# First shift's turns half a chunk later, and forgetting gates of the heads from column tiles

## The chip, the cores and the metric

One core of a Trainium2 chip runs the whole program as a single launch. The metric is the device time of that launch in microseconds (us). TensorE (PE) multiplies matrices into PSUM; ScalarE (ACT), VectorE (DVE) and GpSimd (POOL) do the element work; SyncE (SP) issues the loads of the weights. All data is float32.

## The reference, cut to what matters

256 tokens of width 1024 pass through two blocks of two layers each. The first block's first layer is a differential-attention mixer with a SwiGLU; its activations are shifted and scaled by vectors that come from a conditioning vector `c`:

```
mod_l = split(silu(c) @ ada_w[i] + ada_b[i], 6)     # shift, scale, gate (mixer); shift, scale, gate (ffn)
x = x + mod_l[2] * mixer(...)
x = x + mod_l[5] * swiglu(rmsnorm(x) * (1 + mod_l[4]) + mod_l[3])
```

In the second block each of the two layers has a mixer over one wide projection `h = rms_norm(x) @ w_mix_in` with 3336 columns. The last eight columns are the forgetting logits of the eight attention heads:

```
(..., h_q, h_f, ..., f_q, f_k, f_v, f_f) = split(h)
log_f = log_sigmoid(f_f + f_bias);  cum = cumsum(log_f over tokens)
logit[t, s] = q_t . k_s + cum_t - cum_s              # causal softmax over s
```

The same mixer has an HGRN2 part (`h_q`, `h_f`, ...) whose gates are worked out from 256-column slices of `h`.

## The kernel before, in words

**Products.** Weights stream as 1 MB slabs of 128 x 2048 into a ring of five raw buffers. For each slab ACT makes a rounded copy `hi` (L1277) and DVE the rest `lo` (L1793); both sit in rings of four. PE multiplies activations (also split, `XTh` and `XTl`) with them three times (L458 to L460). A "half chunk" is one slab: four row tiles, two token tiles, three products, 24 matmuls of 512 columns. Each engine's order of work is written out by hand, and the engines wait for each other by semaphores only.

**The first layer's conditioning.** Products of `c` with `ada_w` come as slabs of a quarter matrix. For some (`ada_slab`, L476) PE does them itself with the two columns of `CS` as standing weights, in four column tiles of 32 (L484). For the others (`ada_quarter`, L1809) DVE sums them into `ROW`, eight instructions for a half (L1827, L1830), and PE turns each half of `ROW` into columns by eight matmuls on a matrix of ones (`half_turn`, L505, L517 holds the matmul: four of them, of two passes each). DVE then adds the bias (`half_mods`, L1834, L1842), which frees the next `half_turn` (L511). Half 1 of shift (0, 3) waits for half 0's `half_mods`. The order on PE around the first of these, shift (0, 3), in chunk c == 4 of the first projection, is L622 to L639: the half chunk d+8, both half turns, an `ada_slab`, the half chunk d+9, an `ada_slab`, then the turns of keys and queries (`heads`, L556). On DVE it is L2005 to L2011: two quarters of `ROW`, two `half_mods`, three small instructions (`factor`), and the copy out of PSUM `from_x(4)`.

**The mixer of the second block.** `mix` (PE L1139, ACT L1672, DVE L2467) runs twice. After the first chunk, PE makes the forgetting logits (L1143 to L1147): for each token tile the activations `FULL` (128 x 128) are loaded as standing weights and eight columns of `WF` pass, eight row tiles, so 16 matmuls of eight columns in float32. DVE scales them, adds the bias (L2482), and takes minimum and absolute value (L2486, L2487). Then come the half chunks s = 2 to 11 with small work between. After s == 2 `hgrn_turn` (L1024) turns two slices of `h`; ACT and DVE wait for it (L1685, L2490) and start the chain of the gates (table loads, exponentials, logarithms), which ends for the heads in `LOGS` (L2514). After s == 4 PE sums these over the tokens (`fox_decay`, L1015). `SG` is a buffer that is free at this place; `SEL` (L404, L2356) is a 128 x 8 mask with a one where the partition number mod 32 is the head.

Of the kernel before, what the change touches and what calls it, by code (L numbers as in the profile page):

```python
# [20 lines left out]
P = 128  # L21
D = 1024
KD = D // P
T = 2
# [46 lines left out]
    "hg_decays": "hg_dec hg_tail",  # L71

    "row_squares": "sq sq2 sq_in std std2",
    "exponents": "lam_exp lb_exp",
    "diff_squares": "diff_sq diff_std",
    "hg_logs": "hg_e hg_ln hg_sig hg_z",
    "hg_squares": "hg_rows hg_sq hg_std hg_silu",
# [7 lines left out]
class Counts:  # L85
# [12 lines left out]
    def up(self, name, key=0, step=1):  # L98
        assert (name, key) not in self.table, (name, key)
        shared = SEMAPHORE.get(name, name)  # L100
        self.n[shared] = self.n.get(shared, 0) + step
        self.table[name, key] = self.n[shared]
        return self.sem(name), step

    def at(self, name, key=0):
        return self.sem(name), 1 if self.known is None else self.known[name, key]


def row_tiles(w):
    return w.rearrange("(k p) n -> p k n", p=P)  # L110
# [175 lines left out]
def program(nc, A, out, known):  # L286

    ctx = ExitStack()
    with ctx:
# [4 lines left out]
        def tile_at(name, shape, offset, dt=F32):  # L294
            return nc.alloc_sbuf_tensor_at(name, list(shape), dt, offset=offset)
# [109 lines left out]
        OG = tile_at("OG", [P, HD], gate_at + 11648)  # L405
        FB = tile_at("FB", [P, FOX_H], gate_at + 11904)
        GS = tile_at("GS", [P, T, HALF], gate_at + 11968)
        WF = tile_at("WF", [P, KD, FOX_H], gate_at + 14016)
        FST = tile_at("FST", [P, T, 16], gate_at + 14272)
        LB = tile_at("LB", [P, 8, 2], gate_at + 14528)  # L410
        TRI = tile_at("TRI", [P, 2, P], cst_at)
# [39 lines left out]
        def tensor_engine(pe):  # L451
# [167 lines left out]
            for c in (2, 3, 4):  # L619

                ctx_groups = [(bank[2 + t], CTXh, CTXl, t) for t in range(T)]
                pe.wait_ge(*at("uc_act", (c - 1 if c > 2 else 0, "x")))  # L622
                pe.wait_ge(*at("uc_dve", (c - 1 if c > 2 else 0, "x")))
                half_chunk(d + 2 * c, 0, x_groups_in, False)
                if c == 4:
                    for h in range(2):
                        half_turn(0, 3, h, bank[6])
                    pe.wait_ge(*at("gate_full", (0, 2, 1)))
                    ada_slab(0, 4, 0, bank[7])
                half_chunk(d + 2 * c + 1, 1, x_groups_in, False).then_inc(*up("x_pass", c))  # L630
                if c == 4:
                    ada_slab(0, 4, 1, bank[7])
                    pe.wait_ge(*at("roped", 1280))
                    pe.wait_ge(*at("heads_act", 5))
                    heads(7, bank[4])
                    pe.wait_ge(*at("uc_act", (3, "c")))
                    pe.wait_ge(*at("uc_dve", (3, "c")))
                    pe.wait_ge(*at("heads_act", 6))
                    heads(8, bank[5])  # L639
                if c == 2:  # L640
                    pe.wait_ge(*at("c_hi", 3))
                    pe.wait_ge(*at("c_lo", 3))
                pe.wait_ge(*at("uc_act", (c - 1, "c" if c > 2 else "x")))
                pe.wait_ge(*at("uc_dve", (c - 1, "c" if c > 2 else "x")))
                half_chunk(d + 2 * c, 0, ctx_groups)
                if c == 4:
                    pe.wait_ge(*at("row", (0, 4, 0)))
                    ada_slab(0, 4, 2, bank[7])
                if c == 2:
                    pe.wait_ge(*at("roped", 256))  # L650
                    for n in (0, 1):
                        heads(n, bank[4 + n])
                if c == 3:
                    pe.wait_ge(*at("roped", 768))
                    heads(3, bank[4])
                    heads(4, bank[5])
                    pe.wait_ge(*at("heads_act", 2))
                    half_gate(0, 2, 0, bank[6])
                    half_gate(0, 2, 1, bank[7])
                if c == 4:  # L660
                    pe.wait_ge(*at("heads_act", 8))
                    diff_scores(0)
                half_chunk(d + 2 * c + 1, 1, ctx_groups)
                if c == 4:
                    ada_slab(0, 4, 3, bank[7])
                if c == 2:
                    pe.wait_ge(*at("roped", 512))
                    heads(2, bank[6])
                if c == 3:
                    pe.wait_ge(*at("roped", 1024))  # L670
                    pe.wait_ge(*at("heads_act", 4))
                    heads(5, bank[4])
                    heads(6, bank[5])
                if c == 4:
                    pe.wait_ge(*at("uc_act", (4, "x")))
                    pe.wait_ge(*at("uc_dve", (4, "x")))
                    diff_scores(1)
# [461 lines left out]
            def mix(p):  # L1139
                l, d = MIXES[p], first[f"up{p}"]  # L1140
                first_chunk(p)
                pe.wait_ge(*at("small2", (l, 2)))
                for t in range(T):  # L1143
                    for k in range(KD):
                        last = pe.matmul(bank[7][:, t * FOX_H:(t + 1) * FOX_H], FULL[:, k, tok[t]], WF[:, k, :],
                                         start=(k == 0), stop=(k == KD - 1))
                last.then_inc(*up("fox_z", l))  # L1147
                for s in range(2, 12):
                    c = s // 2
                    if s % 2 == 0 and c >= 2:  # L1150
# [4 lines left out]
                    half_chunk(d + s, s % 2, x_groups(c))  # L1155

                    if s == 2:
                        hgrn_turn(l)
                    elif s == 4:
                        fox_decay(l)  # L1160
                        pe.wait_ge(*at("hg_z", l))
                        pe.wait_ge(*at("hg_k2t", l))
                        hgrn_products(l, 0, K2, Q2, 4)
                    elif s == 6:
                        pe.wait_ge(*at("fox_c", l))
                        hgrn_level(l, 1)
                    elif s >= 7:
                        hgrn_level(l, s - 5)
# [99 lines left out]
        def scalar_engine(act):  # L1268
# [403 lines left out]
            def mix(p):  # L1672
# [6 lines left out]
                                   ACT.Identity, scale=ST[:, 0:1]).then_inc(*up("um_act", (l, c)))  # L1679

                first_chunk(p)
                act.wait_ge(*at("rstd2", p))
                rows_of(0)
                split(d + 5)
# [98 lines left out]
        def vector_engine(dve):  # L1783
# [683 lines left out]
            def mix(p):  # L2467
# [8 lines left out]
                first_chunk(p)  # L2476
                dve.wait_ge(*at("rstd2", p))
                rows_of(0)
                dve.wait_ge(*at("fox_z", l))
                dve.wait_ge(*at("small2", (l, 2)))  # L2480
                for t in range(T):
                    dve.scalar_tensor_tensor(out=FZ[:, 0, t, :], in0=bank[7][:, t * FOX_H:(t + 1) * FOX_H],  # L2482
                                             scalar=ST[:, t:t + 1], in1=FB[:, :], op0=ALU.mult,
                                             op1=ALU.add).then_inc(*up("fox_bias", (l, t)))
                dve.wait_ge(*at("fox_bias", (l, 1)))
                dve.tensor_scalar(FZ[:, 1, :, :], FZ[:, 0, :, :], 0.0, None, ALU.min)  # L2486
                dve.scalar_tensor_tensor(out=FZ[:, 2, :, :], in0=FZ[:, 0, :, :], scalar=-1.0, in1=FZ[:, 0, :, :],  # L2487
                                         op0=ALU.mult, op1=ALU.max).then_inc(*up("fox_abs", l))
                split(d + 5)
                dve.wait_ge(*at("hg_turned", l))  # L2490
                dve.wait_ge(*at("lb", 8))
                dve.tensor_copy(Q2[:, :, :], bank[4][:, :].rearrange("p (k s) -> p k s", k=2)).then_inc(*up("hg_q2t", l))
# [128 lines left out]
        def gpsimd_engine(pool):  # L2621
# [21 lines left out]
            for l in range(2):  # L2643
# [9 lines left out]
                                0.0).then_inc(*up("reset"))  # L2653
                else:
                    pool.wait_ge(*at("added", (5, 1)))
                pool.dma_start(WF[:, :, :], row_tiles(A["w_mix_in_2"][l, :, :])[:, :, MIX_IN - FOX_H:MIX_IN]).then_inc(
                    *up("small2", (l, 0), 16))
                pool.dma_start(FB[:, :], A["fox_f_bias_2"][l, :].partition_broadcast(P)).then_inc(*up("small2", (l, 1), 16))
                pool.dma_start(OG[:, :], A["hgrn_out_gain_2"][l, :].partition_broadcast(P)).then_inc(*up("small2", (l, 2), 16))
# [171 lines left out]
```

## Time and profile before

| | us |
|---|---|
| three runs | 1786.42, 1785.92, 1782.88 (median 1785.92) |
| the profiled execution | 1782.81 |
| its span, first to last instruction | 1781.5 |
| PE busy in the span | 1698.9 (95%) |
| DVE busy | 1104.0 (62%) |
| ACT busy | 807.2 (45%) |
| POOL busy | 48.0 (3%) |

The span is what the trace covers; 1.3 us lie around it. A row of the trace gives start, length, engine, line, operation, output and inputs, the number of instructions merged, and in brackets how long the engine had been idle and what released it. A float32 matmul shows as two records, one for each pass, so a count of records is twice the number of matmuls. The mean granted clock of TensorE over the span is 0.989 of full speed.

### The profile page before, as it was taken

To read this page: it belongs to the slowest core of one execution; us is meant where nothing else is said; L and a number is where in the kernel's file an instruction comes from. 1 tells how busy PE (TensorE), PEld (TensorE's weight loads), DVE (VectorE), ACT (ScalarE), POOL (GpSimd) and SP (SyncE) were. 2 spreads that over 40 slices of the span, in tenths; PEclk is the share of its full clock that TensorE was granted. 3 is DMA by queue.
4 is the path that set the end of the run, shared out by engine and by line. 5 is a ranking of instruction groups with operands and counts; after the bars stand their busy time and mean duration, and the time that the engine had idled before them with its cause. 6 is when DMAs were issued, how large, how long until landed. Compare 5 with 4: busy or idle time off the path is not lost.

```text
span 1781.5 us, 20857 instructions
## 1 busy us (share of the span) xinstructions
PE 1698.9 (95%) x8192; PEld 1375.8 (77%) x8192; DVE 1104.0 (62%) x1284; ACT 807.2 (45%) x968; POOL 48.0 (3%) x60
## 2 busy tenths in 40 slices
PE   6999899999988999999999999999999999999999
PEld 3775678877656887788788788887888788888877
DVE  2876787878657664655546856554655458855542
ACT  3415554333444443464435565443444346664441
POOL 0001000000000000000001200000000003000000
PEclk9999999999989999999999999999999999999999
DMA  9683279887444765565455427655565454336550
GB/s 355 205 279 123 84 257 307 282 293 268 146 135 139 251 233 180 165 194 186 182 165 153 155 72 214 189 188 172 184 189 186 170 168 163 119 99 213 186 187 25
DMA packets 239985, 332.29 MB, mean 187 GB/s; under 512 B 11024, under 2 KB 191988, under 8 KB 239888
## 3 DMA queue, kind: packets, MB, share of 16 engines
q1 hardware_dynamic: 235872, 321.95, 54.4%
q10 hardware_dynamic: 2704, 5.82, 0.9%
q0 software_dynamic: 1312, 3.19, 0.7%
q8 instruction: 66, 1.08, 0.2%
q14 instruction: 31, 0.25, 0.0%
HBM read 329.87 MB, written 1.05 MB: 186 GB/s over the span
## 4 chain that ended last, share of the span: by engine, by line
PE 83%; DVE 10%; ACT 3%; issue 2%; DMA 1%; SPq 0%; DVEq 0%; ACTq 0%
PE bank L458 16%; PE bank L460 16%; PE bank L459 16%; PE bank L789 7%; PE bank L790 7%; PE bank L792 7%; DVE lo L1793 4%; PE bank L887 2%; ACT hi L1277 1%; DMA raw<-in_ada_w 1%; PE bank L1221 1%; PE bank L1222 1%; PE bank L1224 1%; DVE ROW L1830 1%; PE bank L772 1%
## 5 line engine op out<-in xcount | busy, mean ns | idle before, releaser
L1793 DVE TENSOR_TENSOR lo<-raw,hi 128x2048 fp32r<-128x2048 f32 x258 | 591.3, 2295 | 378.9 <-ACT hi L1277 378.6
L1277 ACT ACTIVATE hi<-raw 128x2048 fp32r<-128x2048 f32 x258 | 491.6, 1911 | 333.3 <-PE bank L460 173.8
L458 PE MATMUL bank<-hi,XTh 128*128 128x512 f32 (+1 forms) x1424 | 565.7, 397 | 11.6 <-DVE XTl L1880 4.6
L460 PE MATMUL bank<-hi,XTl 128*128 128x512 f32 (+1 forms) x1424 | 554.1, 389 | 0.0
L459 PE MATMUL bank<-lo,XTh 128*128 128x512 f32 (+1 forms) x1424 | 553.3, 389 | 0.0
L458 PEld LDWEIGHTS bank<-hi,XTh 128*128 128x128 f32 x1424 | 269.2, 189 | 74.3 <-ACT XTh L1293 8.4
L460 PEld LDWEIGHTS bank<-hi,XTl 128*128 128x128 f32 x1424 | 268.6, 189 | 56.4
L459 PEld LDWEIGHTS bank<-lo,XTh 128*128 128x128 f32 x1424 | 269.4, 189 | 52.9 <-issue 1.0
L789 PE MATMUL bank<-hi,HTh 128*128 128x512 f32 x528 | 208.6, 395 | 9.3 <-DVE HTl L1880 9.3
L790 PE MATMUL bank<-lo,HTh 128*128 128x512 f32 x528 | 207.0, 392 | 0.0
L792 PE MATMUL bank<-hi,HTl 128*128 128x512 f32 x528 | 163.5, 391 | 0.0
L789 PEld LDWEIGHTS bank<-hi,HTh 128*128 128x128 f32 x528 | 100.0, 189 | 31.4 <-DVE HTl L1880 10.9
L792 PEld LDWEIGHTS bank<-hi,HTl 128*128 128x128 f32 x528 | 99.7, 189 | 21.1
L790 PEld LDWEIGHTS bank<-lo,HTh 128*128 128x128 f32 x528 | 100.0, 189 | 20.5
L1558 ACT ACTIVATE SG<-bank,ST 128x256 f32<-128x256 f32 x88 | 36.9, 470 | 136.5 <-PE bank L460 136.5
L1830 DVE SCALAR_TENSOR_TENSOR ROW<-raw,CS,ROW 128x512 f32<-128x512 f32 x126 | 94.6, 751 | 4.2
L1293 ACT ACTIVATE XTh<-FULL 128x512 fp32r<-128x512 f32 x44 | 27.4, 632 | 105.7 <-DVE FULL L2160 67.2
L2230 DVE SCALAR_TENSOR_TENSOR HID<-bank,ST,SG 128x256 f32<-128x256 f32 x88 | 38.5, 478 | 55.6 <-ACT SG L1558 55.6
L1880 DVE TENSOR_TENSOR HTl<-bank,HTh 128x512 fp32r<-128x512 f32 x66 | 45.1, 684 | 9.1 <-ACT HTh L1538 9.1
L1558 ACT ACTIVATE SG<-bank 128x256 f32<-128x256 f32 x44 | 14.5, 382 | 71.2 <-PE bank L460 71.2
L1538 ACT ACTIVATE HTh<-bank 128x512 fp32r<-128x512 f32 x66 | 38.5, 583 | 16.3 <-PE bank L887 16.3
L2673 POOL TENSOR_TENSOR hg_e<-hg_BC 128x256 f32<-128x256 f32 x12 | 23.2, 1934 | 641.2 <-DVE hg_BC L2523 620.9
(360 smaller groups left out, 1415.5 us busy)
## 6 DMA issues: line engine op xcount, KB each, us to landing
raw<-in_ffn_w_in SPq DMA_DIRECT2D x176, 512.0 KB, 4.8
raw<-in_ffn_w SPq DMA_DIRECT2D x132, 512.0 KB, 4.9
raw<-in_ada_w SPq DMA_DIRECT2D x96, 512.0 KB, 4.9
raw<-in_ffn_w_out SPq DMA_DIRECT2D x88, 512.0 KB, 4.0
raw<-in_w_mix_in SPq DMA_DIRECT2D x52, 512.0 KB, 4.6
raw<-in_od_pw_w SPq DMA_DIRECT2D x24, 512.0 KB, 4.6
raw<-in_ev_w_in SPq DMA_DIRECT2D x20, 512.0 KB, 9.0
raw<-in_w_mix_out SPq DMA_DIRECT2D x16, 512.0 KB, 4.1
```

Source lines behind the costliest of these rows:

```text
L458: pe.matmul(dst, xh, wh, start=start, stop=False)
L459: pe.matmul(dst, xh, wl, start=False, stop=False)
L460: return pe.matmul(dst, xl, wh, start=False, stop=stop)
L789: pe.matmul(acc[t][m][:, :], sh, w[m][0], start=begin, stop=False)
L790: pe.matmul(acc[t][m][:, :], sh, w[m][1], start=False, stop=False)
L792: last = pe.matmul(acc[t][m][:, :], sl, w[m][0], start=False, stop=end)
L1277: act.activation(hi[r][:, :], raw[g % RAW][:, :], ACT.Copy).then_inc(*up("hi", d))
L1538: act.activation(HTh[:, 2 * c:2 * c + 2, :], b[:, :].rearrange("p (k s) -> p k s", k=2), ACT.Copy).then_inc(*up("ht_hi", (f, c)))
L1558: act.activation(SG[:, t, :], bank[2 * (c % 2) + t][:, 0:HALF], ACT.Silu, scale=1.0 if p in SHIFTED else ST[:, t:t + 1]).then_inc(*up("gat ...
L1793: dve.tensor_tensor(lo[r][:, :], raw[g % RAW][:, :], hi[r][:, :].bitcast(F32), ALU.subtract).then_inc(*up("lo", d))
L1830: m = dve.scalar_tensor_tensor(out=part, in0=w[:, k, :], scalar=CS[:, kk, 0:1], in1=part, op0=ALU.mult, op1=ALU.add)
L1880: dve.tensor_tensor(dst, src, h.bitcast(F32), ALU.subtract).then_inc(*up(name, i))
```

## The change

Three edits. (1) In chunk 4 of the first projection the two half turns of shift (0, 3) stand behind the half chunk d+9 and the `ada_slab` after it, instead of ahead of both; they are still in the same order on DVE. (2) The forgetting logits are made the other way round: eight columns of weights stand still (the tile `CS`, 32 columns wide, of which eight are loaded and 24 are left from before), 256 tokens pass, and row tile k goes to column tile k % 4, so the eight partial products lie in four groups of 32 partitions. ACT copies this 128 x 256 result to `SG`; after the half chunk s == 2 two matmuls with `SG` standing and `SEL` passing sum the four groups and turn tokens to partitions. (3) The instructions of DVE that read the logits move behind the split of slab d+5.

```diff
@@ semaphores
-    "exponents": "lam_exp lb_exp",
+    "exponents": "lam_exp lb_exp fox_zrow",
@@ tiles
-        WF = tile_at("WF", [P, KD, FOX_H], gate_at + 14016)
+        WF = CS
@@ PE, first projection, c == 4
                 half_chunk(d + 2 * c, 0, x_groups_in, False)
                 if c == 4:
-                    for h in range(2):
-                        half_turn(0, 3, h, bank[6])
                     pe.wait_ge(*at("gate_full", (0, 2, 1)))
                     ada_slab(0, 4, 0, bank[7])
                 half_chunk(d + 2 * c + 1, 1, x_groups_in, False).then_inc(*up("x_pass", c))
                 if c == 4:
                     ada_slab(0, 4, 1, bank[7])
+                    for h in range(2):
+                        half_turn(0, 3, h, bank[6])
                     pe.wait_ge(*at("roped", 1280))
@@ PE, mix
                 pe.wait_ge(*at("small2", (l, 2)))
-                for t in range(T):
-                    for k in range(KD):
-                        last = pe.matmul(bank[7][:, t * FOX_H:(t + 1) * FOX_H], FULL[:, k, tok[t]], WF[:, k, :],
-                                         start=(k == 0), stop=(k == KD - 1))
-                last.then_inc(*up("fox_z", l))
+                for k in range(KD):
+                    o = 32 * (k % 4)
+                    last = pe.matmul(bank[7][o:o + 32, 0:S], WF[:, k, :], FULL[:, k, :], start=(k < 4), stop=(k >= 4),
+                                     tile_position=(0, o))
+                last.then_inc(*up("fox_parts", l))
...
                     if s == 2:
+                        pe.wait_ge(*at("masks"))
+                        pe.wait_ge(*at("fox_zrow", l))
+                        for t in range(T):
+                            last = pe.matmul(bank[7][:, S + t * FOX_H:S + (t + 1) * FOX_H], SG[:, 0, tok[t]],
+                                             SEL[:, :].bitcast(F32), start=True, stop=True)
+                        last.then_inc(*up("fox_z", l))
                         hgrn_turn(l)
@@ ACT, mix
                 first_chunk(p)
+                act.wait_ge(*at("fox_parts", l))
+                act.activation(SG[:, 0, :], bank[7][:, 0:S], ACT.Copy).then_inc(*up("fox_zrow", l))
                 act.wait_ge(*at("rstd2", p))
@@ DVE, mix
                 rows_of(0)
+                split(d + 5)
                 dve.wait_ge(*at("fox_z", l))
                 dve.wait_ge(*at("small2", (l, 2)))
                 for t in range(T):
-                    dve.scalar_tensor_tensor(out=FZ[:, 0, t, :], in0=bank[7][:, t * FOX_H:(t + 1) * FOX_H],
+                    dve.scalar_tensor_tensor(out=FZ[:, 0, t, :], in0=bank[7][:, S + t * FOX_H:S + (t + 1) * FOX_H],
...
-                split(d + 5)
@@ POOL
-                pool.dma_start(WF[:, :, :], row_tiles(...)[:, :, MIX_IN - FOX_H:MIX_IN])
+                pool.dma_start(WF[:, :, 0:FOX_H], row_tiles(...)[:, :, MIX_IN - FOX_H:MIX_IN])
```

## Rows read from the trace of the kernel before

**Rows 1.** The page: the chain that ended last, shares by engine

```profile
PE 83%; DVE 10%; ACT 3%; issue 2%; DMA 1%; SPq 0%; DVEq 0%; ACTq 0%
```

**Rows 2.** Timeline of 118 to 136 us, first layer

```profile
118.40 5.54 DVE L1830 SCALAR_TENSOR_TENSOR ROW<-raw,CS,ROW 128x512 f32<-128x512 f32 x7
...
118.71 0.95 PE L517 MATMUL bank<-ONES,ROW 128*128 128x2 f32 x8
...
123.86 0.15 DVE L1842 TENSOR_TENSOR MODS<-bank,COLS 128x4 f32<-128x4 f32 x1
...
124.09 1.85 PE L517 MATMUL bank<-ONES,ROW 128*128 128x2 f32 x8 [4.44 <-DVE MODS L1842]
...
125.87 1.94 PE L484 MATMUL bank<-raw,CS 128*32 128x512 f32 x8
...
134.31 1.06 PE L484 MATMUL bank<-raw,CS 128*32 128x512 f32 x8
135.30 0.66 PE L562 MATMUL bank<-IDENT,UROW 128*128 128x128 f32 x4
```

**Rows 3.** Stretches: us, busy time of PE, PEld, DVE, ACT, POOL, granted clock, DMA share, GB/s

```profile
118.70:124.00 5.30, 0.95 (x9) 0.86 (x7) 5.02 (x8) 0.00 (x0) 0.00 (x0) 0.89 0.72 230
124.00:127.70 3.70, 3.61 (x16) 1.99 (x16) 0.46 (x5) 0.00 (x0) 0.00 (x0) 0.50 1.04 350
127.70:129.70 2.00, 2.00 (x9) 1.58 (x6) 0.00 (x0) 0.00 (x0) 0.00 (x0) 0.52 0.57 164
...
154.00:200.00 46.00, 40.59 (x243) 28.20 (x243) 33.84 (x79) 31.12 (x88) 3.64 (x7) 1.00 0.17 53
```

**Rows 4.** SP's queue at 110 us, and the page's issues (KB, us to landing)

```profile
110.28 0.88 SPq L2696 DMA_DIRECT2D raw<-in_ada_w  x2
...
raw<-in_ada_w SPq DMA_DIRECT2D x96, 512.0 KB, 4.9
```

**Rows 5.** Timeline of the first mixer, 948 to 961 us

```profile
948.85 3.74 PE L1145 MATMUL bank<-WF,FULL 128*128 128x8 f32 x32
949.11 0.69 ACT L1678 ACTIVATE UM<-bank,ST 128x512 f32<-128x512 f32 x1 [0.73 <-PE bank L460]
...
952.44 0.77 PE L458 MATMUL bank<-hi,XTh 128*128 128x512 f32 x1
...
959.51 1.03 PE L1031 MATMUL bank<-IDENT,UM 128*128 128x128 f32 x8
...
960.58 0.69 DVE L2492 COPY hg_Q<-bank 128x512 f32<-128x512 f32 x1 [5.11 <-PE bank L1031]
```

**Rows 6.** Timeline of the second mixer, 1465 to 1476 us

```profile
1465.69 3.63 PE L1145 MATMUL bank<-WF,FULL 128*128 128x8 f32 x32
...
1469.18 0.49 PE L458 MATMUL bank<-hi,XTh 128*128 128x512 f32 x1
...
1474.77 1.04 PE L1031 MATMUL bank<-IDENT,UM 128*128 128x128 f32 x8
```

**Rows 7.** Stretches of the mixers, columns as in Rows 3

```profile
952.40:955.60 3.20, 3.20 (x9) 2.52 (x10) 2.81 (x5) 0.00 (x0) 0.00 (x0) 0.50 0.91 315
...
1469.20:1474.50 5.30, 5.30 (x25) 4.38 (x25) 2.81 (x5) 0.00 (x0) 0.00 (x0) 1.00 0.76 231
```

**Rows 8.** Timeline, PE, 454 to 456 us: 16 records of 256 columns in four tiles

```profile
454.63 1.11 PE L973 MATMUL bank<-TAPW,TAPD 31*81 31x256 f32 x16
455.67 0.50 PE L458 MATMUL bank<-hi,XTh 128*128 128x512 f32 x1
```

**Rows 9.** Timeline of ACT at 973 us: a copy of 128 x 256 out of PSUM

```profile
972.91 0.36 ACT L1706 ACTIVATE NCT<-bank 128x256 fp32r<-128x256 f32 x1
```

**Rows 10.** Timeline at 970 to 972 us: the logs of the gates and their first reader

```profile
970.60 0.41 DVE L2514 TENSOR_TENSOR LOGS<-FZ 128x256 f32<-128x256 f32 x1
...
971.28 0.39 PE L1020 MATMUL bank<-TRI,LOGS 128*128 128x128 f32 x2
```

**Rows 11.** Small work of DVE on the logits, first mixer

```profile
952.62 0.36 DVE L2482 SCALAR_TENSOR_TENSOR FZ<-bank,ST,FB 128x8 f32<-128x8 f32 x2 [1.17 <-PE bank L1145]
```

More of the change, by code:

```diff
@@ L2655, in gpsimd_engine @@
                     pool.wait_ge(*at("added", (5, 1)))
-                pool.dma_start(WF[:, :, :], row_tiles(A["w_mix_in_2"][l, :, :])[:, :, MIX_IN - FOX_H:MIX_IN]).then_inc(
+                pool.dma_start(WF[:, :, 0:FOX_H], row_tiles(A["w_mix_in_2"][l, :, :])[:, :, MIX_IN - FOX_H:MIX_IN]).then_inc(
                     *up("small2", (l, 0), 16))
```

## The prediction

> **What bounds the kernel now.** I read the page first. The chain of work that ended last is PE for 83% and DVE for 10%, and DMA for 1% [rows 1]: PE's instructions in order, broken by short stretches in which another engine is late. So PE time removed counts in full if nothing else is late afterwards, and loads matter little. Then I read the timeline around the two places of the change and the stretches with their granted clock. (About 0.2% of the time, 3.6 us, is what a measurement of this kernel can tell from no change.)
>
> At the first place PE ends half 0's turn (118.71 plus 0.95) and then stands for 4.44 us until DVE's bias add at 123.86 [rows 2]. DVE is not slow at that add, it takes 0.15; it is queued behind the sums of the other half of ROW, 5.54 us from 118.40 [rows 2]. When PE goes on, the clock is at its lower level, 1.2 GHz: 0.50 over 124.0 to 127.7 and 0.52 over 127.7 to 129.7, after 0.89 in the stretch that holds the stand [rows 3]. Everything there costs nearly double: half 1's turn 1.85 against 0.95, a slab product 1.94 against 1.06 [rows 2].
>
> At the second place, twice, PE makes the logits in 32 records (16 matmuls of two passes), from 948.85 to the next chunk's first matmul at 952.44, and from 1465.69 to 1469.18, so 3.59 and 3.49 us [rows 5, 6]. That is 0.109 us a record with only eight columns: loading the 128 x 128 of FULL as weights sets it. In the first mixer the clock is then at 0.50 for 3.2 us, in the second it stays at 1.00 [rows 7], and the chunk behind takes 959.51 less 952.44, 7.07, against 1474.77 less 1469.18, 5.59 [rows 5, 6].
>
> **Edit 1, the half turns moved.** Old, from half 0's turn to the turns of keys: 135.30 less 118.71, 16.59 us [rows 2]. New, in PE's new order at full clock: slab product 0.99 (134.31 to 135.30), half chunk 5.59 (the one at full clock, rows above), slab product 0.99, half 0's turn 0.95, the wait for DVE, half 1's turn 0.95 [rows 2, 6]. The wait: DVE began its add at 123.86 and PE went on at 124.09, 0.23 [rows 2]; DVE is free from 123.86 and half 0 now ends near 127.2, so it is waiting already, with 3.4 us to spare. The bounds of this wait are 0.23 and the old 4.44; I take 0.27. Sum 9.74, **gain 6.85**: of it 4.2 is the stand and the rest the low clock.
>
> Queued behind DVE's adds is from_x(4), which used to run as soon as the half chunk was done and now comes after both, some 3.5 us later relative to that chunk. Its reader is the second pair of scores, after two more half chunks, so it is covered by over 11 us. ACT's copy of ROW now waits for half 0's turn; it is read after the next half chunk, covered too. The first slab product is asked for at 118.7 instead of 125.87: its load was issued at 110.28 and the median landing of such a load is 4.9 [rows 2, 4], so it lands near 116. The slab then frees 7 us sooner and SP issues the next one sooner; SP's queue is in order and nobody is hurt. What is late next? After this place comes attention, where PE, ACT and DVE release each other and the DMA share is 0.17 over 154 to 200 us [rows 3]. No load that was begun before holds a clock of its own there, so the whole sequence should start and end earlier by the same amount.
>
> **Edit 2, the logits by column tiles.** Removed: 3.59 and 3.49. Added: eight matmuls of 256 columns, 16 records in four tiles. The nearest row has this count and width, in row tiles: 16 records of 256 columns from 454.63 to 455.67, **1.04** [rows 8]. The column tiles of the first layer are 8 records of 512 columns in 0.99 [rows 2], the same columns in all, with the same four tiles. Bounds: 0.99 if columns count, 1.98 if records count, and 4.0 if the tiles do not overlap (a 512 wide matmul lasts about 0.99, half of that eight times). I take 1.04 and 0.1 for going in and out of tiles. Added after s == 2: two matmuls, four records with full weights and eight columns, 4 times 0.109, **0.44** [rows 6]. The Trainium skill (TensorEngine Tiling (Array Packing), Instruction Overhead) puts a fixed cost of about 60 cycles on a matmul, whatever its columns below that; by it alone, an estimate, four records would be 0.1 us. The row has four times that for this very shape, and it decides.
>
> Second mixer: 3.49 less 1.14 less 0.44, **gain 1.9**. First mixer: 3.59 less 1.58 is 2.0, and the chunk behind falls from 7.07 to 5.59, 1.48 more, if the clock stays up because the thin stretch of 3.6 us in front of it is gone: **gain 3.5**. Whether it stays up the rows of before can't say; bounds 2.0 and 3.5.
>
> **ACT, DVE, POOL there.** ACT gets one copy of 128 x 256, 0.36 [rows 9], between its last split and the rows of the first chunk. It used to be free for those rows at 949.11 less 0.73 [rows 5]; it now waits for the partial sums until about 950.0, so rows and the next split come some 1.3 us later. The readers of the rows (hgrn_turn) come after 955, the split is for a chunk three chunks away. Its cost is nothing while that cover holds, and 1.3 without it. PE's wait for the copy is 5 us after it. DVE's logits work now starts when the two small matmuls end and runs beside hgrn_turn, which is 1.03 long; the first step takes 0.36 [rows 5, 11] and two shorter ones follow, so DVE is ready when the turn is, where it had idled 5.11 [rows 5]. The split of slab d+5 goes ahead of it and fills that idle time; it ends about 955.0, before the logits at 955.7. The POOL load of the weights has the same pieces into another tile, long before use: nothing.
>
> Does the gain go on from hgrn_turn? ACT and DVE start their gate chain from that turn, and its end, LOGS at 970.60 plus 0.41, meets PE at 971.28, 0.27 us of slack [rows 10]. Both sides start at the same turn, so both move by the same amount and the slack remains. Were the gates started later than the turn, PE would wait here.
>
> **Sum.** 6.85 + 3.5 + 1.9 = 12.25. The profiled execution has 1782.81 (span 1781.5 and 1.3 around it), which gives 1770.6; the median of the runs shown is 3.1 higher, so I forecast **1773.6**.
>
> **Rivals.**
>
> *A, the clock falls all the same.* In edit 1 the two turns (two columns each) and the turns of heads now stand together, 0.95 + 0.27 + 0.95 + some 1.0, a stretch as thin as the logits of the first mixer, after which the clock fell in one of two mixers [rows 7]. If it falls there, a half chunk costs 1.48 more; if it also falls in the first mixer (the small matmuls and the transposes of hgrn_turn, 1.5 us), 1.48 again. Time 1773.6 + 3.0 = 1776.6. Against it: no stand remains, and 256 column products replace the thin ones. Chance 0.16.
>
> *B, column tiles do not overlap for two rounds.* The second round adds onto the same 32 columns, and its weights can enter only when the first lets them. 4.0 instead of 1.04, twice: 1773.6 + 5.9 = 1779.5. The row of four row tiles in two rounds speaks against it [rows 8]. Chance 0.06. The skill (TensorEngine Tiling (Array Packing), Key Properties) adds that a change of tiling mode drains the engine. The trace agrees as far as it can: the tiled group of rows 8 costs 1.04 with its way in and out, so a drain is a tenth and not a microsecond.
>
> *C, edit 1's gain is taken back in the first feed-forward*, where PE, the sums of ROW on DVE and the loads all run close together. If that stage ends when its loads end and those don't start sooner, 6.85 is lost: 1780.4. Against it: its loads start only when PE and the splits free slabs, and attention in between leaves DMA at 0.17 [rows 3]. Chance 0.10. It is still faster by 5.4, 0.3%.
>
> *D, slower.* The place is the end of s == 2 in each mixer: PE stands for ACT's copy, which is in ACT's queue behind a split that waits for its slab. A stand there moves hgrn_turn and with it the gate chain, which has 0.27 to spare [rows 10], and is followed by a stretch of low clock. It decides if the copy comes over 5 us after the partial sums; to end slower than before the stands and their low clock must come to over 6 us in each mixer: 1788. ACT has been free since 948.4, so chance 0.02.
>
> *E, nothing to be seen*: both A and C, and part of B, 1783 to 1786. Chance 0.04.
>
> **How the numbers follow.** The forecast has 0.62. Its own range is 1768 to 1777: 3.1 down if the runs fall where the profiled execution fell, 2 more if stretches of low clock elsewhere fall otherwise, and as much up. A and C are taken in, and B nearly, to 1780; the range 1767 to 1780 leaves out B's end, D and E. Faster by over 0.2%: forecast, A, B and C, 0.94; within 0.2%: 0.04; slower: 0.02.
>
> **What the trace after would show.** Right: the idle time before the second group of turns is near 0.2 instead of 4.44, clock 1.00 from 118 to 136; turns of keys near 128.4; attention as long as before; L1145 gone for a group of 16 records about 1.04 long and one of 4 records of 0.44; hgrn_turn's end 3.5 us and 1.9 us nearer to the first chunk's end; the gate chain reaches PE with the slack unchanged. Wrong: a clock of 0.50 after the turns (A), a group of 4 us (B), a feed-forward that ends where it ended (C), or an idle row of PE released by ACT's SG (D).

## The result and the profile after

The changed kernel took 1772.63 us in the median of four runs (1771.67 to 1773.08); the kernel before, run beside it, 1784.4 (1781.35 to 1786.42, four runs). The ratio is 0.9934, 95% interval 0.9921 to 0.9947. Forecast were 1773.6 and a range of 1767 to 1780. The profiled execution took 1772.36, its span is 1771.1 against 1781.5.

The page of the changed kernel shows busy time by engine and the chain that ended last. The bound is the same engine:

```profile
PE 1696.4 (96%) x8168; PEld 1370.1 (77%) x8168; DVE 1104.2 (62%) x1284; ACT 807.9 (46%) x970; POOL 48.2 (3%) x60
...
PE 84%; DVE 9%; ACT 3%; issue 2%; DMA 1%; SPq 0%; DVEq 0%; ACTq 0%
```

The timeline of PE at edit 1, against [rows 2] (line numbers are those of the changed kernel; L485 is the slab product; L518 the half turns, four matmuls or eight records for each half; L563 the turns of keys):

```profile
123.06 1.06 PE L485 MATMUL bank<-raw,CS 128*32 128x512 f32 x8
124.05 1.05 PE L518 MATMUL bank<-ONES,ROW 128*128 128x2 f32 x8
125.36 1.05 PE L518 MATMUL bank<-ONES,ROW 128*128 128x2 f32 x8 [0.25 <-DVE MODS L1852]
126.27 0.63 PE L563 MATMUL bank<-IDENT,UROW 128*128 128x128 f32 x4
```

The stand of 4.44 us is now 0.25. The turns of keys begin 9.88 us after the first slab product (116.39 in this trace), forecast 9.74, and the old order took 16.59 [rows 2]. The stretches around it, columns as in [rows 3]:

```profile
116.39:124.05 7.66, 7.66 (x41) 4.74 (x40) 4.93 (x7) 0.60 (x1) 0.00 (x0) 1.00 0.82 273
124.05:126.27 2.22, 1.97 (x20) 1.88 (x17) 0.16 (x1) 0.60 (x1) 0.00 (x0) 1.00 1.01 339
126.27:130.20 3.93, 3.93 (x17) 3.34 (x17) 1.04 (x5) 2.99 (x3) 0.00 (x0) 0.57 1.00 369
```

The clock is full through the turns and then falls to its lower level all the same, in the turns of keys and the half chunk behind them. That is the first half of rival A, and it gives part of the gain back.

The timeline of the first mixer, against [rows 5] (L1147 the products in column tiles, L1163 the two small matmuls, L1032 hgrn_turn):

```profile
944.09 0.59 PEld L1147 LDWEIGHTS bank<-FULL,CS 128*32 128x32 f32 x16 [0.35 <-issue]
944.10 1.07 PE L1147 MATMUL bank<-FULL,CS 128*32 128x256 f32 x16
945.23 0.39 ACT L1691 ACTIVATE SG<-bank 128x256 f32<-128x256 f32 x1 [1.71 <-PE bank L1147]
...
948.13 2.29 DVE L1803 TENSOR_TENSOR lo<-raw,hi 128x2048 fp32r<-128x2048 f32 x1 [1.52 <-ACT hi L1285]
...
950.72 0.51 PE L1163 MATMUL bank<-SEL,SG 128*128 128x8 f32 x4
...
951.08 1.07 PE L1032 MATMUL bank<-IDENT,UM 128*128 128x128 f32 x8
951.26 0.36 DVE L2493 SCALAR_TENSOR_TENSOR FZ<-bank,ST,FB 128x8 f32<-128x8 f32 x2 [0.84 <-PE bank L1163]
...
952.19 0.69 DVE L2502 COPY hg_Q<-bank 128x512 f32<-128x512 f32 x1 [0.28 <-PE bank L1032]
```

Sixteen records of 256 columns in 1.07 (forecast 1.04), four small ones in 0.36 from start to start (forecast 0.44); ACT's copy 0.39; DVE is through with the logits 0.28 before it is needed. From the logits' start to hgrn_turn it is 6.98 us, against 10.66 before [rows 5]; about 0.1 more is spent ahead of the group, where the loads of the tiles' weights start late by 0.35. In the first mixer the next chunk starts 1.00 after the group (945.10). In the second mixer L1147 starts at 1457.26 and L1032 at 1464.24, again 6.98, against 9.08 [rows 6].

Where the 10.45 us of difference between the two spans went can be read by setting the same instructions of both traces side by side. I took the starts of ACT's splits (258 in both; the 9th starts at 99.51 in the trace of before, the 13th at 196.75, the 53rd at 459.80, the 65th at 568.96, the 129th at 942.26, the 133rd at 971.11, the 213th at 1463.32, the 217th at 1488.45). Each number below is the time between two of these splits in the changed kernel less the same time in the trace of before, in us. "<99.5" is the time up to the 9th split, "-197" from there to the 13th, and so on:

```
                       start  edit 1   to   to     to    mixer  mix1 to mixer  to     sum
                       <99.5   -197   460   569    942     1    mixer2    2    end
changed kernel         -2.35  -5.08  0.29  2.06   0.23  -3.54  -0.14  -1.98   0.06  -10.45
```

The forecast was -6.85, -3.5 and -1.9 at the three places. The two mixers fit within 0.1. Two parts were not in the sum: 2.35 less before the first edited instruction, and 2.06 more between 460 and 569 us.

### The profile page after: what moved, and what is told of

It is laid out like the page before. It is cut to its first block, busy times and chain, and to the rows that moved or that the text cites. A ratio compares the mean times of both kernels' runs of the same rounds, so it can differ in the third digit from the quotient of the medians.

```text
span 1771.1 us, 20813 instructions
## 1 busy us (share of the span) xinstructions
PE 1696.4 (96%) x8168; PEld 1370.1 (77%) x8168; DVE 1104.2 (62%) x1284; ACT 807.9 (46%) x970; POOL 48.2 (3%) x60
## 4 chain that ended last, share of the span: by engine, by line
PE 84%; DVE 9%; ACT 3%; issue 2%; DMA 1%; SPq 0%; DVEq 0%; ACTq 0%
PE bank L459 17%; PE bank L461 17%; PE bank L460 17%; PE bank L790 7%; PE bank L793 7%; PE bank L791 7%; DVE lo L1803 3%; PE bank L888 2%; DMA raw<-in_ada_w 1%; ACT hi L1285 1%; PE bank L773 1%; PE bank L1229 1%; PE bank L1230 1%; PE bank L1232 1%; PE bank L950 1%
```

## The experiments

The questions are these. Do the two edits add up, each at its own place? Do the fall of the clock behind the turns and the 2.06 us belong to the change? What do the tiles, the delay of half a chunk and DVE's order bring?

The table for all runs first, so that each can be read against it; "clock low" lists where the granted clock was at its lower level from 100 us on, start and length, as recorded in each trace (stretches from 1766 us on, at the very end, are left out). Every row is set against the one profiled execution of the kernel before, that of the rows. The four f kernels ran once each, with the kernel before once beside them, 1780.85 us, so they are read by their traces.

```
                  start  edit 1   to    to    to    mixer  mix1 to mixer   to    sum    clock low from 100 us on (start, length)
                  <99.5   -197   460   569   942     1    mixer2    2     end
kernel before                                                                           123 6.8; 358 3.4; 369 3.4; 509 10.2; 754 3.4; 952 3.4
changed kernel    -2.35  -5.08  0.29  2.06  0.23  -3.54  -0.14  -1.98   0.06  -10.45    127 3.4; 226 3.4; 352 3.4; 362 3.4; 499 13.7; 550 6.8; 748 3.4
a0_again          -2.40  -3.98  0.36  0.57  0.40  -3.56   0.08  -1.97   0.10  -10.40    128 3.4; 148 3.4; 227 3.4; 353 3.4; 363 3.4; 500 13.7; 749 3.4
a0_third           0.75  -6.63 -0.01  0.48  0.27  -3.54  -0.12  -1.96   0.06  -10.71    353 3.4; 363 3.4; 500 13.7; 749 3.4
e1_turns_only     -1.19  -5.09  0.38  2.06  0.27  -1.58  -0.16   3.23  -0.02   -2.10    128 3.4; 227 3.4; 353 3.4; 364 3.4; 500 13.7; 551 6.8; 749 3.4; 1463 6.8
e2_logits_only    -2.33  -0.32 -0.04 -0.07  0.22  -3.55   0.11  -1.97   0.08   -7.87    120 6.8; 355 3.4; 366 3.4; 506 10.2; 751 3.4
e3_turns_split     0.60  -7.14  0.41  0.51  0.05  -3.55  -0.10  -1.97   0.07  -11.11    226 3.4; 353 3.4; 363 3.4; 499 13.7; 749 3.4
e3_again          -0.11  -7.20 -0.02  0.45  0.15  -3.52  -0.15  -1.96   0.08  -12.27    351 3.4; 362 3.4; 498 13.7; 747 3.4
e5_turns_ahead    -2.33  -6.77  0.49  0.49 -0.03  -3.53   0.07  -1.97   0.09  -13.48    224 3.4; 350 3.4; 360 3.4; 497 13.7; 746 3.4
e5_again          -0.34  -5.19  0.43  0.60  0.40  -3.55  -0.24  -1.97   0.02   -9.85    129 3.4; 228 3.4; 354 3.4; 364 3.4; 501 13.7; 750 3.4
f1_one_tile       -1.06  -5.04  0.30  2.10  0.08  -0.74   0.03   0.83   0.05   -3.43    128 3.4; 227 3.4; 354 3.4; 364 3.4; 500 13.7; 552 6.8; 750 3.4
f2_sum_behind     0.20  -4.04  0.46  0.46 -0.04  -3.96   0.53  -2.35   0.60   -8.13    130 3.4; 150 3.4; 229 3.4; 355 3.4; 366 3.4; 502 13.7; 751 3.4
f3_sum_at_once    -1.08  -5.08  0.30  2.13  0.13  -2.89   0.06  -1.33   0.03   -7.75    128 3.4; 227 3.4; 354 3.4; 364 3.4; 500 13.7; 552 6.8; 749 3.4
f4_split_back     -2.26  -5.02  0.25  0.69  0.05  -3.55  -0.22  -1.95   0.12  -11.90    127 3.4; 226 3.4; 352 3.4; 362 3.4; 499 13.7; 748 3.4
```

### Edit 1 alone

```diff
@@ kernel before, PE, c == 4
-                    for h in range(2):
-                        half_turn(0, 3, h, bank[6])
                     pe.wait_ge(*at("gate_full", (0, 2, 1)))
...
                     ada_slab(0, 4, 1, bank[7])
+                    for h in range(2):
+                        half_turn(0, 3, h, bank[6])
```

> Edit 1 alone on the kernel before; the logits stay as they were. Theory (the stand of 4.44 us goes, the low clock moves from the half chunk to the turns of heads): about 5 us faster than before, so 1779 or 0.997; PE waits 0.2 to 0.3 us for the first bias add, the clock is at 0.5 for one stretch behind the turns, and the mixers cost what they cost before (3.6 and 3.5 us for the logits, low clock behind the first). Rival (attention or the first feed-forward take the gain back): no difference, 1784.

Measured: 1778.97 (ten runs) against 1784.29, ratio 0.9968 (0.9957 to 0.9979), so 5.3 us less. In the trace edit 1's place is 5.09 shorter and the wait is 0.25, as in the changed kernel. The rival falls: by 460 us 0.38 is taken back, and 2.06 between 460 and 569 us, which still leaves the kernel clearly faster. One part of the expectation missed: the first mixer kept its clock although its logits were the old ones, and the second lost it for 6.8 us. The stretches of the second mixer of this kernel, columns as in [rows 3], the logits and the chunk behind:

```profile
1459.50:1463.20 3.70, 3.70 (x29) 3.54 (x27) 2.96 (x2) 2.90 (x3) 0.00 (x0) 0.94 0.82 275
1463.20:1470.40 7.20, 7.20 (x25) 6.06 (x24) 2.81 (x5) 0.00 (x0) 0.00 (x0) 0.56 0.61 176
```

That costs 3.23 there, and the first mixer is 1.58 shorter than in the trace of before with the same instructions. So the old logits lose the clock in one of the two mixers in both traces, and which one it is changes. None of the twelve profiles with the new logits has a fall in either mixer.

### Edits 2 and 3 alone

```diff
@@ changed kernel, PE, c == 4
+                    for h in range(2):
+                        half_turn(0, 3, h, bank[6])
                     pe.wait_ge(*at("gate_full", (0, 2, 1)))
...
                     ada_slab(0, 4, 1, bank[7])
-                    for h in range(2):
-                        half_turn(0, 3, h, bank[6])
```

> Edits 2 and 3 alone: the half turns stand where they stood. Theory (PE's path in the two mixers is 3.5 and 2.0 us shorter): 5.5 us faster than before, 1779; the stand of 4.4 us and the low clock near 124 us are there as before. Rival (the gate chain or a split is late and takes part back): 2 us or less, with a wait of PE for LOGS or for a slab in the trace.

Measured: 1777.15 (five runs) against the same 1784.29, ratio 0.9961 (0.9946 to 0.9977), 7.1 us less where 5.5 were expected; the interval reaches from 4.1 to 9.6 and holds both. The trace has 3.55 and 1.97 less in the mixers, and the stand is as it was:

```profile
121.77 1.85 PE L518 MATMUL bank<-ONES,ROW 128*128 128x2 f32 x8 [4.50 <-DVE MODS L1852]
```

The rival falls. The places add up: 5.1 (e1_turns_only) and 5.5 (this kernel), against 10.6 in the three places of the changed kernel. This kernel also has the 2.33 less in the first 99.5 us, where no edit of it lies, and it has neither the low clock near 226 us nor more of it near 500, and no extra time there.

### The changed kernel again

> The changed kernel once more. Every theory expects 1772 to 1773 and the turns of keys near 126 us. Open is the feed of low clock between 480 and 560 us, which was 20.5 us long in the profile of the changed kernel and 10.2 in that of before: if it belongs to the change it is there again with the same length, if it is a matter of the single execution it is not.

> The changed kernel, third time, as the measure for the two beside it. Every theory expects 1771 to 1773. Low clock near 127 us is expected by the theory of the thin stretch (it was there in all executions looked at so far); low clock near 226 us and 13.7 us of it near 499 too, since every kernel with the turns moved had them and the two without did not.

Measured: 1772.14 (four runs, ratio 0.993, 0.9912 to 0.9948) and 1772.04 (six runs, ratio 0.994, 0.9927 to 0.9953). The stretch between 460 and 569 us costs 0.57 and 0.48 more than before in these two, not 2.06. Low clock of 13.7 us near 500 is there in each, the 6.8 us near 550 in neither. So of the 2.06 some 0.5 come with the change and 1.5 with the single execution: the 6.8 us near 550 are in four of the twelve profiles with the turns moved, and these four have the 2.06 to 2.13. In a0_third the clock did not fall behind the turns, although PE had the same wait of 0.26 between them; its turns of keys begin at 129.43:

```profile
126.00:130.00 4.00, 3.75 (x31) 2.62 (x30) 0.52 (x5) 1.19 (x2) 0.00 (x0) 1.00 0.99 345
130.00:134.00 4.00, 4.00 (x22) 3.34 (x20) 1.56 (x4) 2.89 (x3) 0.00 (x0) 1.00 1.01 359
```

Edit 1's place is 6.63 shorter there, where the sum had 6.85. In a0_again it fell twice (127.5 and 148.0) and the place is 3.98 shorter. The same kernel thus gains 4.0, 5.1 or 6.6 us there. The expectation that the falls near 127 and 226 us would be there again failed in a0_third. The fall near 226 us costs less than the others: the column "to 460" is 0.25 to 0.49 in the ten profiles that have it and -0.04 to -0.01 in the three others.

In the first 99.5 us the three executions differ from the one of before by -2.35, -2.40 and +0.75: that part is not the change. It goes with where the clock was low before 100 us. The trace of before has 6.8 us of it from 30.6, and the two executions that are like it (e3_again from 30.5, f2 from 31.0) differ from it by -0.11 and 0.20. The five with 6.8 us from 24 or 3.4 us from 25 differ by -2.26 to -2.40, the three that have 3.4 us twice (from 26 and 50) by -1.06 to -1.19, the two that have it three times by 0.60 and 0.75, and the one with 10.2 us from 26 by -0.34.

### One turn on each side of the slab product

```diff
@@ changed kernel, PE, c == 4
-                    ada_slab(0, 4, 1, bank[7])
-                    for h in range(2):
-                        half_turn(0, 3, h, bank[6])
+                    half_turn(0, 3, 0, bank[6])
+                    ada_slab(0, 4, 1, bank[7])
+                    half_turn(0, 3, 1, bank[6])
```

> The changed kernel with half 0's turn ahead of the slab product and half 1's behind it, so DVE's add is covered by the slab product and the thin work of PE is cut in two. Theory (the thin stretch of turns and transposes is what the clock falls after): clock 1.00 from 118 to 140 us, 0.25 us of wait and up to 1.5 us of low clock gone, 1 to 1.8 us faster than the changed kernel. Rival (the fall hangs on more than this order): only the 0.25 us goes and the clock still falls.

> The kernel with one turn on each side of the slab product, once more, against the changed kernel on the same chip. Theory: no fall of the clock near 127 us again, and 1 to 1.8 us less than the changed kernel in the medians, so 0.9992 of it or less. Rival (the fall there was missing in one execution by luck): a fall of 3.4 us at the place and no difference beyond 0.3 us.

Measured: 1771.11 (four runs, ratio 0.9926, 0.991 to 0.9941) beside 1772.14 of the changed kernel, and 1770.58 (six runs, ratio 0.9922, 0.9907 to 0.9936) beside 1772.04. That is 1.0 and 1.5 us less than the changed kernel on the same chip. The intervals against before overlap, and so do the runs of the first pair; of the second, the six runs (1767.45 to 1771.57) all lie below the six of the changed kernel (1771.62 to 1774.83). PE's timeline of e3_again has no wait between the turns:

```profile
125.20 0.95 PE L518 MATMUL bank<-ONES,ROW 128*128 128x2 f32 x8
126.08 1.06 PE L485 MATMUL bank<-raw,CS 128*32 128x512 f32 x8
127.08 1.05 PE L518 MATMUL bank<-ONES,ROW 128*128 128x2 f32 x8
127.99 0.63 PE L563 MATMUL bank<-IDENT,UROW 128*128 128x128 f32 x4
```

The place is 7.14 and 7.20 shorter than before: 6.85 of the sum and the 0.27 that the sum had for the wait make 7.12. The clock did not fall there in either, as the theory had it; but it did not fall in a0_third either, so two executions can't tell the theory from luck.

### Both turns ahead of the slab product

```diff
@@ changed kernel, PE, c == 4
-                    ada_slab(0, 4, 1, bank[7])
                     for h in range(2):
                         half_turn(0, 3, h, bank[6])
+                    ada_slab(0, 4, 1, bank[7])
```

> The changed kernel with both half turns ahead of the slab product. The wait of 0.25 us between them stays; the slab product now lies between the turns and the transposes of heads. It tells apart what the clock falls after. Theory (a long thin stretch of PE: turns, wait and transposes in a row): no fall near 127 us, edit 1's stretch 1.5 us shorter than in the changed kernel. Rival (the wait between the turns): the fall is there as in the changed kernel.

> The kernel with both turns ahead of the slab product, once more. Theory of the long thin stretch: no fall of the clock near 127 us, edit 1's stretch about 6.8 us shorter than before, 1.5 to 3 us less than the changed kernel's 1772. Rival (luck of single executions): a fall there, and 1771 to 1773.

Measured: 1769.49 (four runs, ratio 0.9921, 0.9907 to 0.9936) and 1771.26 (six runs, ratio 0.9917, 0.9904 to 0.9931). The first profile had no fall behind the turns and 6.77 less at the place, the second had one at 129 us and 5.19 less. So the theory that the fall hangs on the length of the thin stretch is not confirmed: with turns and transposes in a row (the changed kernel, e1 and f1 to f4) the clock fell in seven of eight executions, with the slab product between turns and transposes in one of two, with it between the turns in none of two. These are too few to call the order the cause. What is shown is the price: 1.5 us where it falls once. As versions, both orders with the slab product moved have lower medians than the changed kernel beside them, by 1.0, 1.5 and 2.55 us (1771.11, 1770.58 and 1769.49); the 1771.26 had no changed kernel beside it.

### One column tile instead of four

```diff
@@ changed kernel, mix
-                    o = 32 * (k % 4)
+                    o = 0
                     last = pe.matmul(bank[7][o:o + 32, 0:S], WF[:, k, :], FULL[:, k, :],
-                                     start=(k < 4), stop=(k >= 4), tile_position=(0, o))
+                                     start=(k == 0), stop=(k == KD - 1), tile_position=(0, o))
...
-act.activation(SG[:, 0, :], bank[7][:, 0:S], ACT.Copy)
+act.activation(SG[0:32, 0, :], bank[7][0:32, 0:S], ACT.Copy)
```

The sum then reads 32 partitions of `SG` and of `SEL`.

> The changed kernel with all eight row tiles in one column tile, one after the other; copy and sum read those 32 partitions. It measures what the four tiles bring. Theory (four tiles run beside each other, each product of 256 columns alone takes about 0.43 to 0.5 us): 3.4 to 4.0 us for the group in place of 1.0 to 1.1, so both mixers lose 2.4 to 2.9 us each. Rival (the standing weights of 32 columns are what is cheap, not the tiles): under 1.5 us for the group.

Measured: 1779.38 (one run). The group in the first mixer:

```profile
945.32 3.64 PE L1147 MATMUL bank<-FULL,CS 128*32 128x256 f32 x16
```

3.64 in place of 1.07, the same 16 records. Both mixers lose 2.8 us against the changed kernel (-0.74 less -3.54, and 0.83 less -1.98). The theory holds and the rival falls. Without the tiles the standing weights alone would have been worth next to nothing: 3.64 against the old group's 3.74 [rows 5], and the second mixer is 0.83 longer than before. The first is still 0.74 shorter than in the trace of before because the clock did not fall there, although the group lasts 3.64. So the length of PE's thin group alone does not decide whether the clock falls.

### The small matmuls behind hgrn_turn, and at once

```diff
@@ changed kernel, PE, mix, s == 2: f2_sum_behind_turn
-                        pe.wait_ge(*at("fox_zrow", l))
...
-                        last.then_inc(*up("fox_z", l))
                         hgrn_turn(l)
+                        pe.wait_ge(*at("fox_zrow", l))
...
+                        last.then_inc(*up("fox_z", l))
@@ changed kernel, PE, mix: f3_sum_at_once
                 last.then_inc(*up("fox_parts", l))
+                pe.wait_ge(*at("fox_zrow", l))
...
+                last.then_inc(*up("fox_z", l))
                 for s in range(2, 12):
...
-                        pe.wait_ge(*at("fox_zrow", l))
...
-                        last.then_inc(*up("fox_z", l))
                         hgrn_turn(l)
```

> The changed kernel with the two small matmuls behind the turn of the gates (hgrn_turn) instead of ahead of it. PE's work is the same. DVE then has the logits' small work (0.65 us) and the wait for them ahead of its part of the gate chain. Theory (the chain has 0.27 us to spare at LOGS): DVE starts its copy 0.9 us later relative to the turn, and PE waits 0.3 to 0.9 us for LOGS in each mixer. Rival (ACT's table loads and exponentials set the chain, DVE has room): no wait at LOGS.

Measured: 1774.68 (one run), with the clock low twice behind the turns. No wait of PE at LOGS: hgrn_turn starts at 952.60 and the first reader at 964.86, 12.26 us, where a0_again has 950.86 and 962.68, 11.82; the 0.44 between is the moved work itself. LOGS starts 11.08 after hgrn_turn, in a0_again 11.13, so DVE's late start did not move it. The rival was right that DVE has room. (In the table the first mixer's -3.96 and the 0.53 behind it belong together: the split that divides them came earlier.) DVE's rows of this kernel show why:

```profile
954.01 0.36 DVE L2493 SCALAR_TENSOR_TENSOR FZ<-bank,ST,FB 128x8 f32<-128x8 f32 x2 [1.71 <-PE bank L1164]
...
954.58 0.68 DVE L2502 COPY hg_Q<-bank 128x512 f32<-128x512 f32 x1
...
959.58 0.17 DVE L2514 TENSOR_SCALAR FZ<-FZ 128x16 f32<-128x16 f32 x1 [2.25 <-ACT FZ L1702]
...
963.68 0.41 DVE L2524 TENSOR_TENSOR LOGS<-FZ 128x256 f32<-128x256 f32 x1
```

DVE starts its part 0.91 after ACT's (953.67) and still waits 2.25 us for ACT's exponential of the logits. Up to that point ACT's chain of table loads sets the pace. Behind it DVE does: from 959.58 to LOGS it has no idle time (a split of 2.29 us is in it), while ACT's logarithm of the logits is done at 963.22, 0.46 before LOGS starts.

> The changed kernel with the two small matmuls directly behind the products, ahead of half chunk s == 2. It prices the half chunk of delay. Theory: PE waits for ACT's copy, 0.05 to 0.1 of signal and 0.39 of copy, 0.5 us in each mixer, and nothing else moves: 1 us slower in the two mixers together. Rival (the clock falls at this stand or the stand is longer because ACT is busy with a split): 1 us and more in each.

Measured: 1775.06 (one run). PE stands for ACT's copy:

```profile
947.02 0.58 PE L1153 MATMUL bank<-SEL,SG 128*128 128x8 f32 x4 [0.60 <-ACT SG L1691]
```

The mixers are 0.65 longer each than in the changed kernel (-2.89 less -3.54, -1.33 less -1.98), 1.3 together, where the theory had 0.5 each; the clock did not fall, so the rival did not happen. That is what the half chunk of delay brings.

### DVE's split back behind the logits

```diff
@@ changed kernel, DVE, mix
-                split(d + 5)
                 dve.wait_ge(*at("fox_z", l))
...
                                          op0=ALU.mult, op1=ALU.max).then_inc(*up("fox_abs", l))
+                split(d + 5)
```

> The changed kernel with DVE's split of slab d+5 back behind the logits. Then DVE's 2.3 us of split start only when the small matmuls are done and run into the start of the gate chain. Theory (the order matters): DVE starts its copy for the chain about 1.9 us later than the turn, LOGS comes later and PE waits some 1 to 1.9 us in each mixer. Rival (DVE has over 2 us of room in the chain, waiting for ACT): no wait of PE, the same time as the changed kernel.

Measured: 1770.91 (one run), mixers 3.55 and 1.95 shorter than before, like the changed kernel. The theory falls, the rival holds. The split runs into the chain, and the wait in it takes it up:

```profile
950.37 2.28 DVE L1803 TENSOR_TENSOR lo<-raw,hi 128x2048 fp32r<-128x2048 f32 x1
952.57 0.68 DVE L2502 COPY hg_Q<-bank 128x512 f32<-128x512 f32 x1
...
956.64 0.17 DVE L2514 TENSOR_SCALAR FZ<-FZ 128x16 f32<-128x16 f32 x1 [1.33 <-ACT FZ L1702]
```

DVE's copy is 1.84 later than ACT's (950.73), and DVE waits 1.33 for ACT later on, where it waits 2.72 in a0_again. LOGS starts 11.13 after hgrn_turn in both. Edit 3 is worth nothing here.

## Why the prediction was right, point by point

**The bound.** PE's chain bounds the kernel: right. "Nothing late behind" was right for the mixers (between them -0.14, from the second to the end, 293 us, 0.06) and nearly so for edit 1: 0.29 is lost by 460 us, and about 0.5 between 460 and 569 us, whose cause stays open.

**Edit 1, 6.85.** The order was priced right: 6.63 where the clock stayed up, and 7.14 and 7.20 in the variant without the wait. The wait of 0.27 was 0.25. The step that failed is the full clock behind the turns: in most executions it fell there, in the turns of keys and the chunk behind them, which is the first half of rival A with its 1.48; measured 1.5 (6.63 less 5.08). I gave A a chance of 0.16; its first half, the fall behind the turns, was there in three of four profiles of this order on PE that had nothing else changed or only edit 1, and in all four of f1 to f4. So the forecast time left out what was the usual case. Its second half, a fall in the first mixer, never came.

**Edit 2, 3.5 and 1.9.** Measured 3.54 and 1.98. The group with its way in was 1.10 (1.00 and 0.1) where the sum had 1.04 plus 0.1, the small matmuls 0.36 where it had 0.44. The row with four row tiles [rows 8] was the right neighbour; the bound of 4.0 for tiles that do not overlap was near too, since one tile takes 3.64. The first mixer's 3.5 has 1.5 of clock in it. That this stood in the first mixer is chance: with the same logits e1_turns_only has 1.58 less there and 3.23 more in the second, so against e1 edit 2 gains 1.96 and 5.21. The Trainium skill's rule of a drain between tiling modes (TensorEngine Tiling (Array Packing), Key Properties): the trace agrees with a small one, the 0.35 us before the tiles' first load of weights, of which about 0.1 lengthens PE's path (the group starts 0.32 after the last matmul of the chunk before, where those start 0.23 apart).

**Nothing for ACT, DVE and POOL.** Right, though the margin was misread twice. First, I took the 0.27 us at LOGS as the margin of both engines from the start of the chain; f2 and f4 show that DVE may start 0.9 and 1.8 us late before it is felt, because it waits for ACT's exponential. Behind the exponential it is DVE's own queue that ends in LOGS. Second, 0.27 is counted to the matmul. LOGS is its standing operand, and the load of these weights starts 0.06 after LOGS is done (970.60 plus 0.41):

```profile
971.07 0.41 PEld L1020 LDWEIGHTS bank<-TRI,LOGS 128*128 128x128 f32 x2
```

PE does not wait there: in f2 this load comes 12.03 after hgrn_turn, less the moved 0.44 is 11.59, and it is 11.60 in a0_again, although LOGS is 0.53 early in f2 and 0.06 in a0_again. How late ACT may be was not tried.

**The sum.** 12.25 forecast; 11.8 by the medians beside each other (1784.4 less 1772.63), 10.45 by the two spans. The three places of the change are 10.60 of it (5.08, 3.54, 1.98), 2.35 come from the start, and 2.06 between 460 and 569 us and 0.44 elsewhere go the other way. The stretch from 460 to 569 us was in no rival: some 0.5 us there are in every kernel with the turns moved and not in e2_logits_only, together with 13.7 instead of 10.2 us of low clock near 500 us. C, D, B and E did not happen.

That the time came within 1.0 us of the forecast is partly luck. The forecast counted from a median of 1785.92; with the fourth run beside the changed kernel it is 1784.4. The fall behind the turns and the loss between 460 and 569 us were not in the sum, and the medians still differ by 11.8, 12.15 and 11.3 us in the three measurements of this kernel. By places, without the first 99.5 us, the three executions are 8.1, 8.0 and 11.5 us shorter than the only profiled execution of before. That one is 1.6 us below the median of its kernel; where its other executions lose more is not known.

## What to carry to other kernels

When an engine waits for another that is itself never idle, look at what is queued there ahead of the awaited instruction. Moving the waiting work behind something long that needs neither saves the stand (4.44 us here) and, when the clock then stays up, the low clock behind it.

A thin product (few columns moving, full standing weights) costs its weight loads. Turned round it took 3.64 us in one tile against 3.74 before, and 1.07 in four tiles beside each other.

A gain of a few microseconds is best read from the distance between the same two instructions in both traces, because the whole time also carries falls of the clock elsewhere, 1.5 us for most of them. And one profile of a kernel is one draw of these falls: here three profiles of the same kernel gave 4.0, 5.1 and 6.6 us at the same place.

## What the runs showed of the hardware that was not expected

The granted clock was at its lower level at much the same places in every profile (near 353 and 363, 500, 749 us), but at others it varied from one execution to the next: the same kernel fell once, twice or not at all behind the same instructions (5.08, 3.98 and 6.63 us gained). With old logits the fall was in the first mixer in one trace (3.4 us long) and in the second in another (6.8 us long). The low stretch near 500 us was 13.7 us long in all twelve profiles with the turns moved (4 to 7 us gained at edit 1's place) and 10.2 in both without. Why was not tried. The first 99.5 us differed by up to 3.15 us between executions of the same instructions (-2.40 and 0.75 in the table), and the difference went with the place and number of the low stretches before 100 us. The price of a fall depends on what PE does in it: 1.5 us behind the turns, 0.3 to 0.5 near 226 us.
